# Output projection of a conv and mLSTM encoder: cross products with 16-bit operands, their narrow copies made by ScalarE

## The chip, the core and the metric

The kernel runs on one core of one Trainium2 chip. The metric is the device time of one execution, in microseconds (us); lower is better.

## What is computed

One layer of an encoder on two token groups (256 and 1024 tokens of width 1024): a short gated convolution beside a bidirectional mLSTM, one output projection, and a mixture of 16 experts with expert choice. The change touches the output projection alone:

```python
mlstm_out = jax.nn.sigmoid(o) * ht.reshape(bsz, s, V_W)
mix = jnp.concatenate([conv_out, mlstm_out], axis=-1)
return x + jnp.einsum('bse,ed->bsd', mix, w_out)      # then rms_norm, router, top-k, experts
```

## The kernel before

Five engines run one hand-written program each, in a fixed order, and meet at semaphores. The work has three stages.

1. Input projection (to about 370 us). Each float32 operand is split: a high part rounded to fp32r and a low part (the rest). A product is high x high plus two cross products (high x low, low x high). The cross products of this stage take bf16 operands (`hn_nar`, `wnar`), whose narrow high copies ScalarE makes (line 922).
2. The scan (about 350 to 550 us) over NT = 10 tiles of 128 tokens. For tile n, TensorE makes scores and numerators of the mLSTM, ScalarE scales one direction (`hb`, line 1167), VectorE adds the two (`ht`, line 1614), ScalarE takes their squares (`junkh`, line 1178), VectorE the roots and the gated product `mix`; TensorE transposes `mix` into PSUM (line 2095). ScalarE rounds the high parts of the mix, `conv_high` for slices 0 to 3 (from `cvs`, line 1081) and `heads_high` for slices 4 to 7 (line 1086); VectorE makes the low parts, `conv_low` and `heads_low` (lines 1623, 1651). `project(n, h, k0, k1)` (line 2013) multiplies slices k0 to k1 of tile n with half h of w_out, 512 columns at a time. It is called in pieces, one tile behind the numerators: twelve matmuls a piece in tile 0 (four pieces), then pieces of 2, 2, 4 slices a half. The result `x1` (VectorE's `residual`, line 1556, or ScalarE's `residual_out`, line 1135) is transposed (line 2035), copied to `xT` by ScalarE (line 1094), and multiplied with the router (lines 2050, 2057); token squares are ScalarE's `junk` (line 1109). From tile 8 on VectorE runs the top-k (`choose`).
   w_out is split too: `out_high(k)` on ScalarE (line 1073) and `out_low(k)` on VectorE (line 1573), slices 0 to 3 before the loop, 4 to 7 inside tile 0.
3. The experts (from about 569 us), bound by TensorE and the transfer of the weights.

The order on each engine is that in which the code is written. ScalarE's loop over n calls, for 2 <= n < 8: token_squares(n-2), columns_out(n-2, 1), hb(n), conv_high(n), logit_parts(n-2), squares of the heads (n), softmax_terms, exponentials(n+2), columns_out(n-1, 0), heads_high(n). The inner loop of `project` is this:

```python
for a, (x, w) in enumerate(((xh, wh), (xh, wl), (xl, wh))):
    mm = pe.matmul(psum[:, 6 + h, :], x, w,
                   start=(k == 0 and a == 0), stop=(k == KD - 1 and a == 2 and not with_x))
```

## Time and profile before

| | |
|---|---|
| runs shown | 1290.13, 1288.26, 1289.65 us; median 1289.65 |
| profiled execution | 1287.62 us, span 1285.9 us |
| TensorE matmul busy | 1249.5 us (97%) |
| VectorE, ScalarE, GpSimd busy | 904.5 us (70%), 743.2 us (58%), 320.9 us (25%) |
| mean granted TensorE clock | 0.992 |
| chain that ended last | TensorE 91%, VectorE 3%, issue 2%, ScalarE 2% |
| line 2013 (output projection) | 480 matmuls, 9% of the chain |

The page lists busy time per engine, the chain of work that ended last, and the costliest groups. In a timeline each row is a start, a length, the engine, the line, and what is written from what. Matmuls overlap, so the distance between starts tells the cost of one, not its length.

### The profile page before, as it was taken

How to read it: one execution, taken by the hardware profiler on the slowest of the kernel's cores; microseconds unless marked ns; L12 is line 12 of the kernel's file. 1: busy time of each engine (PE TensorE's matmuls, PEld its weight loads, DVE VectorE, ACT ScalarE, POOL GpSimd, SP SyncE). 2: the span in 40 equal slices, each digit the busy share in tenths (PEclk: the TensorE clock that was granted, in tenths of full speed). 3: DMA queues.
4: the chain of work that ended last, by engine and by line, in shares of the span. 5: the costliest groups of instructions: out<-in, count | busy, mean ns of one | idle time of the engine just before them, and what ended most of it. 6: DMA issues, size and time to landing. Idle time of an engine off the chain costs nothing.

```text
span 1285.9 us, 25128 instructions
## 1 busy us (share of the span) xinstructions
PE 1249.5 (97%) x9766; PEld 1026.7 (80%) x9818; DVE 904.5 (70%) x1293; ACT 743.2 (58%) x1082; POOL 320.9 (25%) x316
## 2 busy tenths in 40 slices
PE   8999999999999999889999999999999999999994
PEld 7868996666688888678988898888889888988893
DVE  6462122442487555989888887888798889888887
ACT  7645322223345454468667766766776667667765
POOL 2512221010143331141232213231314131223040
PEclk9999999999999999989999999999999999999997
DMA  8231544360279774199999999999999999999997
GB/s 276 67 123 51 167 145 129 119 178 10 94 214 283 213 210 138 56 304 369 346 305 311 316 338 297 310 325 333 296 318 333 319 301 316 344 303 309 296 347 282
DMA packets 242176, 314.76 MB, mean 245 GB/s; under 512 B 16112, under 2 KB 206064, under 8 KB 242112
## 3 DMA queue, kind: packets, MB, share of 16 engines
q1 hardware_dynamic: 226720, 268.54, 63.4%
q0 software_dynamic: 15392, 45.36, 12.0%
q8 instruction: 42, 0.69, 0.2%
q14 instruction: 22, 0.18, 0.1%
HBM read 274.41 MB, written 39.44 MB: 244 GB/s over the span
## 4 chain that ended last, share of the span: by engine, by line
PE 91%; DVE 3%; issue 2%; ACT 2%; DMA 1%; POOL 1%; SPq 0%; POOLq 0%; ACTq 0%; DVEq 0%
PE psum L2301 23%; PE psum L2162 15%; PE psum L2308 11%; PE psum L2013 9%; PE psum L2324 9%; PE psum L2129 8%; PE psum L2342 4%; PE psum L2333 4%; PE psum L2075 1%; PE psum L2294 1%; PE psum L2080 1%; PE psum L2035 1%; PE psum L1993 1%; PE psum L2027 1%; DVE eraw L1919 1%
## 5 line engine op out<-in xcount | busy, mean ns | idle before, releaser
L1846 DVE TENSOR_TENSOR elo<-eraw,ehi 128x2048 bf16<-128x2048 f32 x192 | 433.2, 2283 | 1.2 <-ACT ehi L1240 1.2
L1240 ACT ACTIVATE ehi<-eraw 128x2048 fp32r<-128x2048 f32 x192 | 362.2, 1902 | 22.5 <-PE psum L2342 17.3
L2301 PE MATMUL psum<-xc,ehi 128*128 128x320 f32 x2048 | 330.4, 313 | 1.5 <-DVE xc L1851 1.5
L2301 PEld LDWEIGHTS psum<-xc,ehi 128*128 128x128 f32 x2048 | 302.3, 188 | 3.0 <-DVE xc L1851 1.8
L2308 PE MATMUL psum<-xb,elo 128*128 128x160 bf16 x2048 | 163.9, 233 | 0.0
L1859 DVE TENSOR_REDUCE gu<-psum 128x320 f32<-128x640 f32 x128 | 104.9, 820 | 78.0 <-PE psum L2308 77.9
L2308 PEld LDWEIGHTS psum<-xb,elo 128*128 128x128 bf16 x2048 | 138.5, 98 | 13.1
L2162 PE MATMUL psum<-hn_nar,wnar 128*128 128x512 bf16 (+1 forms) x748 | 141.2, 343 | 1.2
L2324 PE MATMUL psum<-ehi,hc 128*128 128x512 f32 x512 | 132.6, 406 | 0.0
L2162 PEld LDWEIGHTS psum<-hn_nar,wnar 128*128 128x128 bf16 x768 | 73.0, 98 | 63.0 <-issue 4.5
L2324 PEld LDWEIGHTS psum<-ehi,hc 128*128 128x128 f32 x512 | 95.1, 188 | 22.2
L1402 DVE SCALAR_TENSOR_TENSOR wnar<-wraw,g1c,whi 128x256 bf16<-128x256 f32 x96 | 40.0, 486 | 100.6 <-ACT whi L930 100.5
L1304 ACT ACTIVATE sg<-gu 128x320 f32<-128x320 f32 x64 | 30.2, 472 | 135.8 <-DVE gu L1859 135.8
L2129 PE MATMUL psum<-hn_hi,whi 128*128 128x512 f32 (+1 forms) x384 | 83.6, 367 | 0.0
L824 POOL DMA_INDIRECT acc_s<-yt,idx x15 | 24.1, 1605 | 222.8 <-ACT yp L1261 192.9
L2129 PEld LDWEIGHTS psum<-hn_hi,whi 128*128 128x128 f32 x384 | 63.5, 188 | 12.1 <-issue 0.3
L2162 PE MATMUL psum<-wnar,hn_nar 128*128 128x256 bf16 (+1 forms) x608 | 71.7, 274 | 1.0 <-DVE hn_nar L1377 0.6
L930 ACT ACTIVATE whi<-wraw,g1c 128x256 fp32r<-128x256 f32 x92 | 38.0, 496 | 50.1 <-PE psum L2129 48.6
L2013 PE MATMUL psum<-woh,mxh 128*128 128x512 f32 x160 | 66.5, 416 | 0.2 <-ACT xT L1094 0.2
L2162 PEld LDWEIGHTS psum<-wnar,hn_nar 128*128 128x128 bf16 x608 | 57.7, 98 | 9.7 <-issue 1.0
L2013 PE MATMUL psum<-woh,mxl 128*128 128x512 f32 x160 | 62.7, 392 | 0.0
L2013 PE MATMUL psum<-wol,mxh 128*128 128x512 f32 x160 | 62.4, 390 | 0.0
(294 smaller groups left out, 1652.8 us busy)
## 6 DMA issues: line engine op xcount, KB each, us to landing
eraw<-in_w_gate_dram SPq DMA_DIRECT2D x64, 1024.0 KB, 9.6
eraw<-in_w_up_dram SPq DMA_DIRECT2D x64, 1024.0 KB, 8.1
eraw<-in_w_down_dram SPq DMA_DIRECT2D x64, 1024.0 KB, 12.5
wraw<-in_w_in_dram SPq DMA_DIRECT2D x12, 1024.0 KB, 7.4
negm<-negm_d SPq DMA_DIRECT2D x10, 512.0 KB, 6.9
v<-v_d SPq DMA_DIRECT2D x18, 256.0 KB, 4.0
xa<-in_x_sample_dram SPq DMA_DIRECT2D x8, 512.0 KB, 6.8
xs<-in_x_sample_dram SPq DMA_DIRECT2D x8, 512.0 KB, 5.0
```

The lines of the kernel that those rows point to most:

```text
L1240: act.activation(f["ehi"][:, j % RING, :], f["eraw"][:, raw_slot(s, j), :], ACT.Copy).then_inc(S["ehi"], 1)
L1402: w = dve.scalar_tensor_tensor(wnar[j % 2][:, LOW, k, 0:CH], b["wraw"][:, j % 2, k, :], b["g1c"][:, k:k + 1], whi[j % 2][:, k, 0:CH].bitca ...
L1846: dve.tensor_tensor(f["elo"][:, j % RING, :], f["eraw"][:, raw_slot(s, j), :], f["ehi"][:, j % RING, :].bitcast(F32), ALU.subtract).then_i ...
L1859: dve.tensor_reduce(f["gu"][:, (i // 2) % 2, i % 2, :, :], both, AX_X, ALU.add).then_inc(S["gu_add"], 1)
L2013: mm = pe.matmul(psum[:, 6 + h, :], x, w, start=(k == 0 and a == 0), stop=(k == KD - 1 and a == 2 and not with_x))
L2129: mm = pe.matmul(result(i), lhs, rhs, start=(first and k == 0), stop=(not first and k == KD - 1))
L2162: mm = pe.matmul(result(i), lhs, rhs, start=(first and k == 0 and of_x == LOW), stop=(not first and k == KD - 1 and of_x == HIGH))
L2301: pe.matmul(o[:, 0:2 * NC], hi[:, k, c], x[:, k, :, :].rearrange("p a t -> p (a t)"), start=(k == 0), stop=False, skip_group_check=True)
L2308: mm = pe.matmul(o[:, NC:2 * NC], lo[:, k, c], xb[:, k, :], start=False, stop=(k == KD - 1), skip_group_check=True)
L2324: mm = pe.matmul(psum[:, 4 + h, :], f["hc"][:, 2 * q + kk, a, :], f["ehi"][:, j % RING, full_columns(kk, h)], start=(q == 0 and kk == 0 an ...
L2333: pe.matmul(psum[:, 4 + h, :], f["hbf"][:, 2 * q + kk, :], f["elo"][:, j % RING, full_columns(kk, h)], start=False, stop=False, skip_group ...
L2342: mm = pe.matmul(psum[CAPP * i:CAPP * (i + 1), 6, 0:CH], f["hid"][:, k, CAPS:NC], f["eraw"][:, raw_slot(s, j), c], start=(k == 0), stop=(k ...
```

## The change

The low parts of w_out and of the mix become bf16, and a narrow bf16 copy of each high part is added beside them: `wol` becomes `won` and `mxl` becomes `mxn`, each with room for both in the same bytes. ScalarE makes the narrow copies: `out_weights_narrow(k)` eight times (128x1024) and `mix_narrow(n, k0)` twice a tile (128x512). In `project` all high products of a call come first, then all its cross products, with waits for the narrow copies between. The high products and the number of matmuls stay as they are.

```diff
@@ -230,14 +230,14 @@
         d = {}
-        for specs in ([("mxh", [P, KD, T], F32R), ("mxl", [P, KD, T], F32R)],
-                      [("woh4", [P, KD, T], F32R), ("wol4", [P, KD, T], F32R)],
+        for specs in ([("mxh", [P, KD, T], F32R), ("mxn", [P, KD, 2 * T], BF16)],
+                      [("woh4", [P, KD, T], F32R), ("won4", [P, KD, 2 * T], BF16)],
                       [("cvs", [P, KD, T], F32), ("woraw4", [P, KD, T], F32)]):
             d.update(stage_buffers(specs))
         d.update(overlay(size(HN[:1]), ("og", [P, KD, T], F32)))
         d.update(overlay(at_weights, ("woraw0", [P, 4, D], F32)))
-        d.update(overlay(at_weights, ("wol0", [P, 4, D], F32R)))
+        d.update(overlay(at_weights, ("won0", [P, 4, 2 * D], BF16)))
         d.update(overlay(at_weights + 2 * SLOT, ("woh0", [P, 2, D], F32R)))
         d.update(overlay(at_weights + 3 * SLOT + WIDE, ("woh2", [P, 2, D], F32R)))
@@ -264,7 +264,7 @@
         QUARTERS = SP_ // KD
         spare_col = d["router"][:, 2, SP_ - 1:SP_]
         mxh = d["mxh"][:, 2:4, SP_:T].rearrange("p s (k t) -> p s k t", k=KD)
-        mxl = d["mxl"][:, 0:2, SP_:T].rearrange("p s (k t) -> p s k t", k=KD)
+        mxn = d["mxn"][:, 0:2, 2 * SP_:2 * T].rearrange("p s (a k t) -> p s a k t", a=2, k=KD)
         cvs = d["cvs"][:, 1, SP_:T].rearrange("p (s k t) -> p s k t", s=2, k=4)
         og = d["og"][:, 2, SP_:T].rearrange("p (s n) -> p s n", s=2)
         g2b = d["g2b"][:, :]
@@ -279,9 +279,9 @@
                 return d[("woh0", "woh2")[k // 2]][:, k % 2, :]
             return d["woh4"][:, k, SP_:T]
-        def out_lo(k):
-
-            return d["wol0"][:, k, :] if k < 4 else d["wol4"][:, k, SP_:T]
+        def out_narrow(k, a):
+
+            return d["won0"][:, k, a * D:(a + 1) * D] if k < 4 else d["won4"][:, k, 2 * SP_ + a * D:2 * SP_ + (a + 1) * D]
         HALF2, PROMPT = 32, 64
         SEL = PROMPT + NE
@@ -1073,6 +1073,17 @@
                 act.activation(out_hi(k), out_raw(k), ACT.Copy, scale=d["hgc"][:, k - 4:k - 3] if k >= 4 else 1.0
                                ).then_inc(S["wo_hi"], 1)
+            def out_weights_narrow(k):
+
+                act.wait_ge(S["wo_lo"], k + 1)
+                act.activation(out_narrow(k, HIGH), out_hi(k).bitcast(F32), ACT.Copy).then_inc(S["wo_nar"], 1)
+
+            def mix_narrow(n, k0):
+
+                act.wait_ge(S["mxh_done"], 2 * n + (1 if k0 == 0 else 2))
+                act.activation(mxn[:, n % 2, HIGH, k0:k0 + 4, :], mxh[:, n % 2, k0:k0 + 4, :].bitcast(F32), ACT.Copy
+                               ).then_inc(S["mx_nar"], 1)
+
             def conv_high(n):
                 act.wait_ge(ld_mix[n % 2], 16 * 2 * (n // 2 + 1))
@@ -1140,6 +1151,8 @@
                 out_high(k)
             for n in range(3):
                 exponentials(n)
+            for k in range(4):
+                out_weights_narrow(k)
             for n in range(NT + 2):
                 if n == NT:
@@ -1167,10 +1180,16 @@
                         i = act.activation(d["hb"][:, h, :], psum[:, 3 + h % 2, VPAD * (h // 2):VPAD * (h // 2) + DV],
                                            ACT.Copy, scale=d["sm"][:, n % 2, 4 + by_half(h):5 + by_half(h)])
                     i.then_inc(S["hb_done"], 1)
+                    if n == 1:
+                        for k in range(4, KD):
+                            out_weights_narrow(k)
+                        mix_narrow(0, 4)
                     if n >= 1:
                         conv_high(n)
                     if n >= 2:
                         logit_parts(n - 2)
+                    if n >= 1:
+                        mix_narrow(n, 0)
                     act.wait_ge(S["ht_done"], n + 1)
                     if n >= 1:
                         act.wait_ge(S["hsum"], n)
@@ -1180,6 +1199,7 @@
                     i.then_inc(S["hsum"], 1)
                     if n == 0:
                         conv_high(0)
+                        mix_narrow(0, 0)
                         for k in range(4, KD):
                             out_high(k)
                 if n == NT - 1:
@@ -1196,6 +1216,8 @@
                     columns_out(n - 1, 0)
                 if n < NT:
                     heads_high(n)
+                    if n > 0:
+                        mix_narrow(n, 4)
                 if n == NT - 1:
                     residual_out(n - 1, 1)
                     scaled_tokens(LATE)
@@ -1570,7 +1592,7 @@
             def out_low(k):
                 dve.wait_ge(S["wo_hi"], k + 1)
-                dve.scalar_tensor_tensor(out_lo(k), out_raw(k), d["hgc"][:, k - 4:k - 3] if k >= 4 else 1.0,
+                dve.scalar_tensor_tensor(out_narrow(k, LOW), out_raw(k), d["hgc"][:, k - 4:k - 3] if k >= 4 else 1.0,
                                          out_hi(k).bitcast(F32), ALU.mult, ALU.subtract).then_inc(S["wo_lo"], 1)
             def router_weights():
@@ -1620,7 +1642,7 @@
                 s = n % 2
                 dve.wait_ge(S["mxh_done"], 2 * n + 1)
-                dve.tensor_tensor(mxl[:, s, 0:4, :], cvs[:, s, :, :], mxh[:, s, 0:4, :].bitcast(F32), ALU.subtract
+                dve.tensor_tensor(mxn[:, s, LOW, 0:4, :], cvs[:, s, :, :], mxh[:, s, 0:4, :].bitcast(F32), ALU.subtract
                                   ).then_inc(S["cvl_done"], 1)
             def head_roots(n):
@@ -1648,7 +1670,7 @@
             def heads_low(n):
                 dve.wait_ge(S["mxh_done"], 2 * n + 2)
-                dve.tensor_tensor(mxl[:, n % 2, 4:8, :], psum[:, 5, :].rearrange("p (k t) -> p k t", k=4),
+                dve.tensor_tensor(mxn[:, n % 2, LOW, 4:8, :], psum[:, 5, :].rearrange("p (k t) -> p k t", k=4),
                                   mxh[:, n % 2, 4:8, :].bitcast(F32), ALU.subtract).then_inc(S["mxl_done"], 1)
             def last_roots():
@@ -2002,16 +2024,24 @@
                     pe.wait_ge(S["xT_done"], 2 * (n - 1) + h + 1)
                 c = slice(512 * h, 512 * h + 512)
                 with_x = joint(n) and (n, h) != (NS, 0)
+                if n == 0:
+                    pe.wait_ge(S["wo_hi"], k1)
+                if k1 == KD:
+                    pe.wait_ge(S["mxh_done"], 2 * n + 2)
                 for k in range(k0, k1):
-                    if n == 0:
-                        pe.wait_ge(S["wo_lo"], k + 1)
-                    if k == 4:
-                        pe.wait_ge(S["mxl_done"], n + 1)
-                    xh, xl = mxh[:, n % 2, k, :], mxl[:, n % 2, k, :]
-                    wh, wl = out_hi(k)[:, c], out_lo(k)[:, c]
-                    for a, (x, w) in enumerate(((xh, wh), (xh, wl), (xl, wh))):
-                        mm = pe.matmul(psum[:, 6 + h, :], x, w,
-                                       start=(k == 0 and a == 0), stop=(k == KD - 1 and a == 2 and not with_x))
+                    pe.matmul(psum[:, 6 + h, :], mxh[:, n % 2, k, :], out_hi(k)[:, c], start=(k == 0), stop=False)
+                if n == 0:
+                    pe.wait_ge(S["wo_lo"], k1)
+                    pe.wait_ge(S["wo_nar"], k1)
+                if k0 == 0:
+                    pe.wait_ge(S["mx_nar"], 2 * n + 1)
+                if k1 == KD:
+                    pe.wait_ge(S["mxl_done"], n + 1)
+                    pe.wait_ge(S["mx_nar"], 2 * n + 2)
+                for k in range(k0, k1):
+                    for of_x, of_w in ((HIGH, LOW), (LOW, HIGH)):
+                        mm = pe.matmul(psum[:, 6 + h, :], mxn[:, n % 2, of_x, k, :], out_narrow(k, of_w)[:, c], start=False,
+                                       stop=(k == KD - 1 and of_x == LOW and not with_x))
                 if k1 == KD:
                     if with_x:
                         pe.wait_ge(ld_x[n % 2], 16 * (n // 2 + 1))
```

TensorE, the start of tile 0's projection: four transposes of the heads, the scores of tile 2, then two pieces. Before (operands w_out high or low, mix high or low; two slices of the first piece):

```order
L2027 MATMUL psum<-qz,kTs 128x128 x4
L2013 MATMUL psum<-woh,mxh 128x512
L2013 MATMUL psum<-wol,mxh 128x512
L2013 MATMUL psum<-woh,mxl 128x512
L2013 MATMUL psum<-woh,mxh 128x512
L2013 MATMUL psum<-wol,mxh 128x512
```

Now (all four pieces of tile 0, up to the numerators of tile 2):

```order
L2057 MATMUL psum<-qz,kTs 128x128 x4
L2032 MATMUL psum<-woh,mxh 128x512 x4
L2043 MATMUL psum<-won,mxn 128x512 x8
L2032 MATMUL psum<-woh,mxh 128x512 x4
L2043 MATMUL psum<-won,mxn 128x512 x8
L2032 MATMUL psum<-woh,mxh 128x512 x4
L2043 MATMUL psum<-won,mxn 128x512 x8
L2032 MATMUL psum<-woh,mxh 128x512 x4
L2043 MATMUL psum<-won,mxn 128x512 x8
L2105 MATMUL psum<-vs,SD 128x129 x8
```

The triples are sorted into runs of four high and eight cross products; each run of eight stands behind the waits for `wo_lo`, `wo_nar`, `mx_nar` and, in the third piece, `mxl_done`.

ScalarE from the squares of tile 0 to those of tile 1. Before:

```order
L1178 ACTIVATE junkh,ms<-ht 128x128 x4
L1081 ACTIVATE mxh<-cvs 128x512
L1073 ACTIVATE woh<-woraw,hgc 128x1024 x4
L1086 ACTIVATE mxh<-psum 128x512
L1167 ACTIVATE hb<-psum,sm 128x128 x4
L1081 ACTIVATE mxh<-cvs 128x512
L1178 ACTIVATE junkh,ms<-ht 128x128 x4
```

Now:

```order
L1197 ACTIVATE junkh,ms<-ht 128x128 x4
L1092 ACTIVATE mxh<-cvs 128x512
L1084 ACTIVATE mxn<-mxh 128x512
L1073 ACTIVATE woh<-woraw,hgc 128x1024 x4
L1097 ACTIVATE mxh<-psum 128x512
L1180 ACTIVATE hb<-psum,sm 128x128 x4
L1079 ACTIVATE won<-woh 128x1024 x4
L1084 ACTIVATE mxn<-mxh 128x512
L1092 ACTIVATE mxh<-cvs 128x512
L1084 ACTIVATE mxn<-mxh 128x512
L1197 ACTIVATE junkh,ms<-ht 128x128 x4
```

Between `hb(1)` and the squares of tile 1 stand four copies of 128x1024 and two of 128x512 more than before.

ScalarE in the last tile, n = 9. Before:

```order
L1094 ACTIVATE xT<-psum 128x512
L1086 ACTIVATE mxh<-psum 128x512
L1135 ACTIVATE x<-psum 128x512
L1117 ACTIVATE tk<-x,ms 128x1024
L1094 ACTIVATE xT<-psum 128x512
```

Now:

```order
L1105 ACTIVATE xT<-psum 128x512
L1097 ACTIVATE mxh<-psum 128x512
L1084 ACTIVATE mxn<-mxh 128x512
L1146 ACTIVATE x<-psum 128x512
L1128 ACTIVATE tk<-x,ms 128x1024
L1105 ACTIVATE xT<-psum 128x512
```

The narrow copy of the last four slices stands between the high copy and the residual `x`.

## Rows read from the trace of the kernel before

**Rows 1.** The page: busy time of TensorE (section 1) and the chain (section 4).
```profile
PE 1249.5 (97%) x9766; PEld 1026.7 (80%) x9818; DVE 904.5 (70%) x1293; ACT 743.2 (58%) x1082; POOL 320.9 (25%) x316
...
PE 91%; DVE 3%; issue 2%; ACT 2%; DMA 1%; POOL 1%; SPq 0%; POOLq 0%; ACTq 0%; DVEq 0%
```

**Rows 2.** Windows, one round of the scan; us, busy of PE, PEld, DVE, ACT, POOL, clock, DMA.
```profile
439.75:457.00 17.25, 17.25 (x121) 14.44 (x120) 10.40 (x36) 8.74 (x29) 5.29 (x8) 1.00 0.74 214
```

**Rows 3.** Timeline of TensorE, tile 0; columns: start, length, instruction.
```profile
376.45 0.39 PE L2013 MATMUL psum<-wol,mxh 128*128 128x512 f32 x1
...
380.31 0.39 PE L2013 MATMUL psum<-woh,mxh 128*128 128x512 f32 x1
...
385.75 0.94 PE L2075 MATMUL psum<-vs,SD 128*128 128x129 f32 x7
```

**Rows 4.** Runs of bf16 (timeline) and fp32r products (chain) before the scan.
```profile
359.99 3.40 PE L2162 MATMUL psum<-hn_nar,wnar 128*128 128x512 bf16 x15
```

```profile
348.82 3.68 PE psum L2129 x16
```

**Rows 5.** Timelines of ScalarE and VectorE in tile 0.
```profile
376.99 1.15 ACT L1073 ACTIVATE woh<-woraw,hgc 128x1024 fp32r<-128x1024 f32 x1 [0.41 <-DMA woraw<-in_w_out_dram]
...
378.52 1.14 ACT L1167 ACTIVATE hb<-psum,sm 128x128 f32<-128x128 f32 x4
...
384.00 0.31 ACT L1178 ACTIVATE junkh<-ht 128x128 f32<-128x128 f32 x1 [3.09 <-DVE ht L1614]
```

```profile
379.26 2.47 DVE L1573 SCALAR_TENSOR_TENSOR wol<-woraw,hgc,woh 128x1024 fp32r<-128x1024 f32 x2
```

**Rows 6.** ScalarE copies: a run in the timeline, and one form of the groups.
```profile
339.25 3.90 ACT L1073 ACTIVATE woh<-woraw 128x1024 fp32r<-128x1024 f32 x4 [21.01 <-PE psum L2129]
```

```profile
L922 ACT ACTIVATE wnar<-whi 128x2048 bf16<-128x2048 f32 x12 | 22.9, 1910 | 0.3
```

**Rows 7.** The chain in tile 1; columns: start, length, what.
```profile
390.98 0.60 ACT xT L1094
...
393.64 0.64 PE psum L2050 x16
```

**Rows 8.** Timelines of ScalarE, VectorE and TensorE in a steady round.
```profile
430.57 0.18 ACT L1178 ACTIVATION_READ_ACCUMULATOR junkh<-ht 128x1 f32 x1
...
443.41 0.60 ACT L1094 ACTIVATE xT<-psum 128x512 f32<-128x512 f32 x1 [1.83 <-PE psum L2035]
```

```profile
430.94 0.17 DVE L1356 TENSOR_SCALAR ms<-ms 128x5 f32<-128x5 f32 x1
...
434.49 0.68 DVE L1556 TENSOR_TENSOR x<-psum,xs 128x512 f32<-128x512 f32 x1
```

```profile
436.10 0.60 PE L2035 MATMUL psum<-ident,x 128*128 128x128 f32 x4
```

**Rows 9.** Timelines of ScalarE and VectorE in the last tile.
```profile
526.95 0.60 ACT L1086 ACTIVATE mxh<-psum 128x512 fp32r<-128x512 f32 x1 [3.44 <-PE psum L2095]
527.44 0.59 ACT L1135 ACTIVATE x<-psum 128x512 f32<-128x512 f32 x1
```

```profile
521.31 0.28 DVE L1796 COPY AFF<-psum 16x128 f32<-16x128 f32 x1
```

**Rows 10.** Windows of TensorE (busy, clock, DMA), and its first instruction behind two stops.
```profile
526.90:528.10 1.20, 0.02 (x2) 1.00 0.00 0
543.00:546.00 3.00, 0.95 (x16) 1.00 0.56 176
...
547.00:555.00 8.00, 5.38 (x29) 0.57 1.04 349
...
1271.00:1272.00 1.00, 0.54 (x2) 0.73 1.03 418
```

```profile
549.76 0.60 PE L2268 MATMUL psum<-ident,aff 128*16 128x128 f32 x2 [2.62 <-DVE aff L1675]
```

```profile
1271.44 0.54 PE L2399 MATMUL psum<-spare 128*128 128x1 f32 x2 [2.06 <-ACT psum L1338]
```

More of the change, by code:

```diff
@@ L339, in hybrid_conv_mlstm_moe @@
             "ld0 ld1 ldm0 ldm1 ld_mix0 ld_mix1 ld_x0 ld_x1 padded qs_done s_ps e_exp e_done sd_done num_ps router "
-            "den_done hb_done ht_done hsum mix_done mixT_ps mxh_done mxl_done o_ps x1_done "
+            "den_done hb_done ht_done hsum mix_done mixT_ps mxh_done mxl_done wo_nar mx_nar o_ps x1_done "
             "x1_out0 x1_out1 sum2 tk_done tk_out0 tk_out1 xT_ps2 xT_done "
```

## Prediction

> **What bounds the kernel now.** I read the page first, then the chain of waits, then each engine's timeline in the scan stage, the only stage that the change touches. TensorE is busy for 97% of the span and makes 91% of the chain that ended last [rows 1]: the reader should see that a microsecond of TensorE time is worth a microsecond nearly everywhere. One round of the scan (17.25 us) has TensorE busy for all of it, ScalarE for 8.74 and VectorE for 10.40 [rows 2]. So work can be added to ScalarE for nothing, but only where nobody stands waiting for the instruction behind it. There are three places in the scan where somebody does.
>
> **Part 1, the cross products.** There are 10 tiles x 2 halves x 8 slices x 2 = 320 of them. In the middle of a run of full-width fp32r products TensorE starts one every (385.75 - 376.45) / 41 = 0.2268 us [rows 3]. The same shape in bf16 runs elsewhere in this kernel: 15 records in 3.40 us from the first start to the last end, where one takes 0.379, so (3.40 - 0.38) / 14 = 0.216 us [rows 4]. That gives 320 x 0.011 = 3.5 us. The busy means (about 390 against 379 ns) would say the same; the pitch is what counts, since matmuls overlap. The 160 high products now start in runs of 2 or 4 right behind 16-bit ones; a run of 16 such in the input projection goes at 3.68 / 16 = 0.230 us [rows 4], so they lose 160 x 0.003 = 0.5. I take **-3.0 us**. Ends: -3.5 if the high ones keep 0.2268; -2.4 if besides the first cross product behind each high run keeps the fp32r pitch (4 + 9 x 6 = 58 runs x 0.011 = 0.6).
> The rows show fp32r at 227 and bf16 at 216 ns. The Trainium skill (TensorE: Matmul & The Clock Gate, Back-to-back issue gap) gives a warm isolated gap of N / 2.4 + 2.5 ns whatever the type, 216 ns at 512 columns; by that alone this part would be worth nothing, and the trace agrees only for bf16.
>
> **Part 2, the copies that TensorE waits for.** In tile 0 the order is: hb(1), then the four narrow copies of w_out slices 4 to 7, then the narrow copy of the four head slices of mix, and the third call of project (half 0, slices 4 to 7) needs all five before its first cross product. ScalarE starts hb(1) at 378.52 and is through with issuing it at 379.52 (four instructions of 1.14 in all, the last overlapping by 0.14) [rows 5]. A copy of 128x1024 costs (3.90 - 1.05) / 3 = 0.95 us in a run [rows 6]; a bf16 result makes it no faster (128x2048 takes 1.910) [rows 6]. VectorE has the last low part ready at 379.26 + 2.47 = 381.73 [rows 5], before the fourth copy would start at 379.52 + 3 x 0.95 = 382.37. Then the mix copy starts at 383.3 and takes 0.63: **ready at 383.9**. TensorE reaches the third call at 380.31 [rows 3], less 16 x 0.011 = 0.2, and its four high products take 0.9: **it is there at 381.05**. It stands still for **+2.9 us**. Nothing of TensorE's can pass the wait: 20 matmuls and the next round's numerators (385.75 [rows 3]) are queued behind it. Ends: +2.3 (only the last copy and the mix copy behind the low part of 381.73: 1.05 + 0.5), +3.7 (each copy at 1.15, the length of one with a scale column [rows 5]).
>
> **Part 3, the same copies on the way to the squares.** conv_high(1) and the first narrow copy of tile 1 stand behind those five. VectorE's head sums are done at 384.0, where ScalarE's squares start [rows 5]; now conv_high starts at 383.8, its narrow copy 0.65 later, and the squares 0.5 after that, at 385.0. That is 1 us later on a path that has to meet a TensorE 2.7 us later: free. The four copies for slices 0 to 3 wait for VectorE's low parts and end some 0.4 us after ScalarE would have begun hb(0); the last eviction of the stage waits for TensorE, so this is free too.
>
> **Part 4, one link in tile 1.** The chain from TensorE's transposes at 390.98 to the router product at 393.64 is all ScalarE: xT, mxh, junk, xT [rows 7]. The narrow copy of tile 1's head slices now stands between mxh and junk. It waits for mxh's own completion, 0.1, and issues for 0.5: **+0.6 us**. Ends 0.5 and 0.75.
>
> **Part 5, the steady rounds.** The copy ahead of the squares delays them by 0.4; they ended at 430.75 and VectorE began the roots at 430.94 (it waits for the logits as well), so 0.2 us reach it. The residual behind the roots is there at 434.49 + 0.68 = 435.17, and TensorE takes it up 0.9 us later [rows 8]: covered. The copy ahead of junk uses up 0.6 of the 1.83 us that ScalarE waits for xT [rows 8]. Cost 0; if that cover were gone it would be up to 0.6 a round.
>
> **Part 6, one link at the end.** In the last tile mxh at 526.95 is followed at once by x (residual, 527.44), for which TensorE's transposes wait [rows 9]. The narrow copy goes between: **+0.6 us**. VectorE's top-k chain began at 521.31 when TensorE's affinities came [rows 9]; the two chains reach the first gather within some 0.2 us of each other. So the 0.6, less the 0.4 that TensorE gains on its last 66 matmuls, is seen in full.
>
> **Sum without the clock:** -3.0 + 2.9 + 0.6 + 0.6 = +1.1 us. VectorE's instructions, the queues of SP and GpSimd and all transfers keep their order and sizes; they only shift.
>
> **Part 7, the clock.** The granted clock fell to its lower level, 1.2 of 2.4 GHz, twice here: at 547.8, after a stretch of few and small products (busy 0.95 of the 3 us from 543), and at about 1271.45, when TensorE had stood still for 2.06 us behind dense work [rows 10]. Idle spells of 1.2 us (526.9 [rows 10]) left it alone. The new stop of 2.9 us is longer than the one that was followed by a fall. A mean of 0.57 over the eight microseconds from 547 [rows 10] is 6.8 us at half speed, from 547.8 to 554.7 or 4.9 us beyond TensorE's return at 549.76. Ends: 0, and 4.9 / 2 = 2.5 us. I take 2.8 us of busy low time, so **+1.4 us**, since what resumes here are full-width products and not 128-column transposes.
> The Trainium skill (TensorE: Matmul & The Clock Gate, Why this matters for your kernels) asks for no idle gaps over about 3 us between bursts; by that the gap of 2.9 just escapes and the sum stays +1.1. This speaks for rival B.
>
> **The cases.** A change of 0.2% is 2.6 us; less than that can't be told from none. The profiled execution took 1287.62 us (span 1285.9), 2.0 under the median of 1289.65; I add the sum to the median.
> - **A, forecast, 0.42:** the stop and one short fall of the clock, +2.5: **1292.1 us**. It lies just under the bound, so about half of its chance is slower.
> - **B, the stop without a fall, 0.25:** +1.1: 1290.8. For it: nothing shows that every stop of 2 us brings a fall. Against: the 2.06 us before 1271.44.
> - **C, the clock stays low for long, 0.13:** the other side, slower. Place: the stop at 381 to 384. It decides if the low level lasts as long as it did behind 549.76: 1.1 + 2.5 = +3.6, and +4.6 if the copies take 1.2 us each: 1293.3 to 1294.3.
> - **E, ScalarE becomes the bound in the steady rounds, 0.08:** if the two copies a round reach TensorE by 0.5 us each in 8 rounds, +4.0 on top of 1.1: 1294.8. From 1.83 us of wait down to nothing it would take three times the copy that I count; against.
> - **D, the gain without the stop, 0.10:** if ScalarE's copies are over before TensorE is there (each 128x1024 under 0.3 us), only -3.0 + 1.2 = -1.8; together with a pitch of 0.216 for the high products as well (160 x 0.014 = 2.2 and 0.5 more), -4.5: 1285.2. Nothing in rows 6 supports copies that fast.
> - The change doing something else than it says (0.02) is out by the order of instructions: 320 products of mxn with won are there.
>
> Faster by over 0.2%: D without its smaller half and a little for what I do not see, 0.09. Slower: half of A, C, E, 0.40. Within: 0.51. The range takes A, B and C with the bounds of parts 1, 2 and 7: 1288.3 to 1294.5.
>
> **What would show it.** Right: cross products at 379 ns and 0.216 apart; TensorE idle once for about 2.9 us near 381, released by ScalarE's narrow copy of mix; the granted clock under 1.00 within 3 us of that; in later rounds no wait of TensorE, and a round of about 16.95 us; 28 more ScalarE copies, 8 of some 1.04 and 20 of some 0.6 us. Wrong: a stop under 1.5 us or none; rounds that don't get shorter (the pitch was not the type's), or longer ones (E); a wait for wo_lo in place of the copies.

## The result and the profile after

| | before | after |
|---|---|---|
| median of 13 runs each | 1288.15 us | 1292.54 us |
| range of them | 1287.58 to 1290.13 | 1290.74 to 1294.45 |
| ratio, 95% interval | | 1.0029 [1.0022, 1.0037] |
| profiled execution, its span | 1287.62, 1285.9 | 1292.54, 1290.8 |

The change makes the kernel slower: by 0.29% or 3.7 us by the ratio, by 4.4 us between the two medians. Twice more, on other occasions, the ratio was 1.0022 and 1.0026.

The page of after, sections 1, 4 and 5 (against [rows 1]):

```profile
PE 1251.7 (97%) x9818; PEld 994.4 (77%) x9818; DVE 904.6 (70%) x1293; ACT 761.5 (59%) x1110; POOL 320.6 (25%) x316
...
PE 89%; DMA 3%; DVE 3%; ACT 2%; issue 2%; POOL 1%; SPq 0%; POOLq 0%; ACTq 0%; DVEq 0%
...
L2043 PE MATMUL psum<-won,mxn 128*128 128x512 bf16 x320 | 80.0, 384 | 3.0 <-ACT mxn L1084 3.0
```

The first row has 28 more ScalarE instructions and 18 us more of its time, while weight loads lose 32 us. The chain has 3% DMA, which before had 1%; three transfers are new in it, and two of them are shown below. The last row is the group of the cross products: its one idle time is a stop of 3.0 us for the narrow copy of mix.

TensorE's timeline in tile 0 (against [rows 3]):

```profile
381.20 1.28 PE L2032 MATMUL psum<-woh,mxh 128*128 128x512 f32 x4
385.51 2.68 PE L2043 MATMUL psum<-won,mxn 128*128 128x512 bf16 x8 [3.03 <-ACT mxn L1084]
387.63 2.27 PE L2032 MATMUL psum<-woh,mxh 128*128 128x512 f32 x4
```

Four high products take 1.28 us ahead of the stop and 2.27 behind it, so the clock fell. Windows of after across that place, and one steady round; us, busy of PE, PEld, DVE, ACT, POOL, granted clock, DMA (against [rows 2]):

```profile
386.00:387.00 1.00, 1.00 (x5) 0.39 (x4) 0.61 (x1) 1.00 (x5) 0.00 (x0) 0.73 1.32 167
387.00:390.00 3.00, 3.00 (x8) 1.67 (x7) 1.88 (x12) 3.00 (x14) 0.00 (x0) 0.52 1.03 348
390.00:391.00 1.00, 1.00 (x6) 0.49 (x5) 0.96 (x3) 0.05 (x1) 0.88 (x2) 1.00 1.12 344
428.31:445.24 16.93, 16.93 (x120) 11.10 (x119) 10.40 (x36) 9.76 (x31) 5.28 (x8) 1.00 0.79 219
```

The clock is at its lower level, 1.2 of 2.4 GHz, from about 386.5 to 390. The round is 16.93 us instead of 17.25, TensorE busy for all of it, although ScalarE has 1.0 us more to do.

The way to the stop, in the chain of waits of after:

```profile
12.07 7.41 DMA xa<-in_x_sample_dram
...
368.84 9.54 DMA woraw<-in_w_out_dram
...
379.46 0.57 ACT mxh L1097
380.04 1.03 ACT hb L1180 x4
381.07 3.78 ACT won L1079 x4
384.85 0.53 ACT mxn L1084
...
385.51 2.68 PE psum L2043 x8
```

The chain of after has 36.8 us of DMA, that of before 16.6. The transfer of w_out is 9.5 of them and leads to the stop: ScalarE runs without a pause from its landing to the fifth copy, and TensorE stands behind it. The first row shown is another matter. The input x lands at 19.5 us, after ScalarE has waited 0.8 us for it, and TensorE then waits 1.47 us for ScalarE's `hn_hi` at 23.8, against 0.34 at 22.6 in before. From there on this execution runs 1.2 us late, long before the first line that the change touches (the third of the new transfers, 7.9 us of `wraw`, stands before this one).

ScalarE in tile 1 (against [rows 7]) shows the link:

```profile
397.06 0.59 ACT L1097 ACTIVATE mxh<-psum 128x512 fp32r<-128x512 f32 x1
397.69 0.63 ACT L1084 ACTIVATE mxn<-mxh 128x512 bf16<-128x512 f32 x1
398.22 1.04 ACT L1120 ACTIVATE junk<-x 128x1024 f32<-128x1024 f32 x1
```

Before, mxh at 391.48 was followed by junk at 391.95, 0.47 us later. Now it is 1.16.

**Stages of the program.** From the timelines I took when TensorE begins each tile's numerators (tile 1: T1), the first router product, the last projection, and GpSimd's first gather of rows for the experts (`xg`). Each difference is a stage, in us:

| kernel | T1 | T1 to T2 | to router | to T3 | T3 to T9 | to last projection | to gather | to end |
|---|---|---|---|---|---|---|---|---|
| before | 370.47 | 15.28 | 7.89 | 11.59 | 103.50 | 32.98 | 20.05 | 724.14 |
| after | 371.69 | 19.83 | 8.36 | 11.49 | 101.58 | 33.08 | 20.35 | 724.44 |
| difference | +1.22 | +4.55 | +0.47 | -0.10 | -1.92 | +0.10 | +0.30 | +0.30 |

The differences add up to 4.9 us, the difference of the two spans. T1 to T2 holds the stop and the fall of the clock; the six rounds from T3 to T9 give back 0.32 us each. The first column is the late landing of x; it and the last column were in no part of the prediction.

### The profile page after: what moved, and what is told of

The parts are those of the page before. It is cut to its first block, busy times and chain, and to the rows that moved or that the text cites. A ratio compares the mean times of both kernels' runs of the same rounds, so it can differ in the third digit from the quotient of the medians.

```text
span 1290.8 us, 25232 instructions
## 1 busy us (share of the span) xinstructions
PE 1251.7 (97%) x9818; PEld 994.4 (77%) x9818; DVE 904.6 (70%) x1293; ACT 761.5 (59%) x1110; POOL 320.6 (25%) x316
## 4 chain that ended last, share of the span: by engine, by line
PE 89%; DMA 3%; DVE 3%; ACT 2%; issue 2%; POOL 1%; SPq 0%; POOLq 0%; ACTq 0%; DVEq 0%
PE psum L2331 23%; PE psum L2192 15%; PE psum L2338 11%; PE psum L2354 9%; PE psum L2159 8%; PE psum L2043 5%; PE psum L2372 4%; PE psum L2363 4%; PE psum L2032 3%; PE psum L2324 1%; PE psum L2105 1%; PE psum L2110 1%; DMA woraw<-in_w_out_dram 1%; PE psum L2065 1%; PE psum L2015 1%
## 5 line engine op out<-in xcount | busy, mean ns | idle before, releaser
L2192 PE MATMUL psum<-hn_nar,wnar 128*128 128x512 bf16 (+1 forms) x768 | 143.8, 344 | 0.0
L2043 PE MATMUL psum<-won,mxn 128*128 128x512 bf16 x320 | 80.0, 384 | 3.0 <-ACT mxn L1084 3.0
L2363 PE MATMUL psum<-elo,hbf 128*128 128x512 bf16 x256 | 66.4, 382 | 0.0
L2372 PE MATMUL psum<-eraw,hid 128*32 128x256 f32 x1024 | 61.9, 382 | 0.0
```

The costliest lines, as they stand in the source:

```text
L2043: mm = pe.matmul(psum[:, 6 + h, :], mxn[:, n % 2, of_x, k, :], out_narrow(k, of_w)[:, c], start=False, stop=(k == KD - 1 and of_x == LOW a ...
L2192: mm = pe.matmul(result(i), lhs, rhs, start=(first and k == 0 and of_x == LOW), stop=(not first and k == KD - 1 and of_x == HIGH))
L2363: pe.matmul(psum[:, 4 + h, :], f["hbf"][:, 2 * q + kk, :], f["elo"][:, j % RING, full_columns(kk, h)], start=False, stop=False, skip_group ...
L2372: mm = pe.matmul(psum[CAPP * i:CAPP * (i + 1), 6, 0:CH], f["hid"][:, k, CAPS:NC], f["eraw"][:, raw_slot(s, j), c], start=(k == 0), stop=(k ...
```

## Experiments

Each kernel's expectation stands as it was recorded. All ratios are to the kernel before on the same chip. The stage to T3 is left out here: 11.50 to 11.60 us.

| kernel | median us | ratio, 95% interval | T1 | T1 to T2 | to router | T3 to T9 | to last proj. | to gather | to end |
|---|---|---|---|---|---|---|---|---|---|
| types_only | 1287.89 | 0.9985 [0.9976, 0.9994] | 370.96 | 15.75 | 7.71 | 101.56 | 32.45 | 20.74 | 725.73 |
| copies_only | 1295.73 | 1.0056 [1.0041, 1.0070] | 370.47 | 21.45 | 8.36 | 103.48 | 33.67 | 19.96 | 724.13 |
| ungrouped | 1295.09 | 1.0047 [1.0034, 1.0060] | 370.60 | 22.19 | 8.36 | 102.48 | 33.30 | 20.17 | 724.58 |
| fill | 1293.64 | 1.0037 [1.0025, 1.0049] | 370.73 | 18.21 | 8.37 | 101.58 | 33.10 | 20.67 | 725.86 |
| change_again | 1292.08 | 1.0022 [1.0011, 1.0032] | 371.42 | 20.28 | 8.36 | 101.56 | 33.10 | 20.59 | 725.89 |
| links | 1290.93 | 1.0015 [1.0006, 1.0024] | 372.83 | 20.63 | 7.70 | 101.56 | 32.45 | 20.79 | 726.05 |
| nostop | 1289.09 | 0.9998 [0.9989, 1.0007] | 370.62 | 16.45 | 9.77 | 101.58 | 33.10 | 19.95 | 724.77 |
| both | 1288.04 | 0.9989 [0.9980, 0.9998] | 371.00 | 16.12 | 8.58 | 101.56 | 32.45 | 20.60 | 724.54 |
| fill_again | 1293.67 | 1.0034 [1.0022, 1.0046] | 370.47 | 18.37 | 8.36 | 101.56 | 33.11 | 20.27 | 727.27 |
| change_third | 1292.91 | 1.0026 [1.0017, 1.0035] | 371.29 | 17.80 | 8.36 | 101.58 | 33.09 | 19.95 | 725.84 |
| both_again | 1288.70 | 0.9993 [0.9984, 1.0002] | 371.32 | 15.66 | 8.60 | 101.56 | 32.46 | 20.59 | 724.43 |
| before_again | 1289.34 | 1.0002 [0.9992, 1.0012] | 370.40 | 15.28 | 8.14 | 103.48 | 32.99 | 20.00 | 724.17 |

### The two halves of the change: types_only and copies_only

types_only has the change's order and 16-bit operands, but no narrow copies and no waits for them. Its cross products multiply the low part of mix with the low part of w_out in both places, so this part of the projection is another sum.

```diff
-for k in range(4): out_weights_narrow(k)
-mix_narrow(...)
-pe.wait_ge(S["wo_nar"], k1); pe.wait_ge(S["mx_nar"], ...)
-pe.matmul(..., mxn[:, n % 2, of_x, k, :], out_narrow(k, of_w)[:, c], ...)
+pe.matmul(..., mxn[:, n % 2, LOW, k, :], out_narrow(k, LOW)[:, c], ...)
```

> The changed kernel without ScalarE's narrow copies and their waits; both cross products multiply the low parts (low x low), so the cross products are left out of the result while their number, shape and type stay. Theory (the gain is the 16-bit pitch, the loss is the copies): no stop near 381, the clock stays at its upper level there, each steady round 16.93 us against 17.25, and the whole is 3.0 to 3.5 us faster than before (ratio 0.9973 to 0.9977). Rival (16-bit products or their grouping cost something themselves, such as a slower high product or a slower start behind a wait): equal to before or slower, ratio 1.000 or more.

copies_only is the kernel before with the change's order, copies and waits; the copies go to memory that nobody reads (ScalarE's squares also wait for the first of them, which are long done), and all products stay fp32r.

```diff
+for k in range(4): out_weights_narrow(k)   # and all other calls, as in the change
-pe.matmul(..., mxn[:, n % 2, of_x, k, :], out_narrow(k, of_w)[:, c], ...)
+pe.matmul(..., (mxh, mxl)[..., k, :], (out_lo, out_hi)(k)[:, c], ...)   # fp32r
```

> The kernel before with all products in fp32r, high ones first in each call as in the change, and the 28 narrow copies made by ScalarE at the same places into unused memory, with the same waits of TensorE. Theory: the stop near 381 is there with 2.8 to 3.1 us, in most executions the clock falls behind it (1.7 us), the link in tile 1 (0.5) and the one in the last tile (0.6) too; rounds stay at 17.25 us; 5.5 to 7 us slower than before. Rival (the copies are hidden, the loss has to do with the 16-bit operands): within 2 us of before.

The two halves come apart in the table. The types alone give the whole gain of the rounds (101.56 against 103.50) and neither link (7.71 and 32.45). The copies alone leave the rounds at 103.48, so ScalarE's copies of 0.63 us, two a round, cost the steady rounds nothing; the copies carry the stop (21.45) and both links (8.36, and 33.67 against 32.98).

The expectation for types_only, 3.0 to 3.5 us faster than before, was missed: the ratio gives 1.9 us (0.8 to 3.1). Its trace shows why. From T1 to the last projection it takes 168.97 us against 171.24, 2.3 less, and that holds a wait of 0.56 us in tile 0 for VectorE's low part of w_out that before doesn't have; so the shorter products are worth 2.8 us up to there. From T9 to the gather it takes 53.19 us against 53.03: the 0.5 us gained on the last tile is not seen at the gather (see links). copies_only, 7.2 us slower by the ratio (5.3 to 9.0), was expected at 5.5 to 7. The stop, in the waits of TensorE from 350 to 600 us of copies_only, and the clock behind it:

```profile
PE psum L2066 <- ACT free L1104: 3.0, 1, 3.0
```

```profile
383.00:391.00 8.00, 6.62 (x17) 5.20 (x18) 5.91 (x23) 5.89 (x20) 1.28 (x2) 0.57 1.10 299
```

Eight microseconds at a mean of 0.57 are a low stretch twice as long as in after, and T1 to T2 is 1.6 us longer than in after.

### Grouping: ungrouped

```diff
-for k in range(k0, k1):
-    pe.matmul(psum[:, 6 + h, :], mxh[...], out_hi(k)[:, c], ...)
 ...
 for k in range(k0, k1):
+    pe.matmul(psum[:, 6 + h, :], mxh[...], out_hi(k)[:, c], ...)
     for of_x, of_w in ((HIGH, LOW), (LOW, HIGH)):
```

> The changed kernel with the old order inside a call: high, cross, cross for each slice. The waits for the copies come before the first high product. Theory (a product behind one of the other type takes the fp32r pitch, and high products ahead of the stop are work done in its shadow): rounds of 17.05 us or more (10 more changes of type a round at 0.011), the stop 0.9 us longer, 1.8 to 2.0 us slower than the change. Rival (order of the types is free): rounds as in the change, 16.93 us, and only the 0.9 us of the stop.

The wait of TensorE (its waits from 350 to 575 us) is 1.6 us longer than in after:

```profile
PE psum L2040 <- ACT mxn L1084: 4.6, 1, 4.6
```

Four high products that no longer run ahead of it make 0.9 of that, as expected. The other 0.7, which was not, is when things came: T1 is 1.1 us earlier than in after and the last slice of w_out 0.4 earlier.

The rounds tell more. With each fp32r product between 16-bit ones they take 102.48 / 6 = 17.08 us against 16.93 grouped and 17.25 with one type. Grouped, a round has its 16 high products in 6 runs (pieces of 2 or 4 slices), ungrouped in 16, so 10 more turns from one type to the other and back cost 0.15 us, some 0.015 each. Grouping is worth nearly half of what the types give.

### The clock behind the stop: fill, fill_again, change_again and change_third

fill keeps TensorE busy in the stop with 24 transposes to PSUM columns that nobody reads any more.

```diff
 if n == 0:
+    if (h, k0) == (0, 4):
+        pe.wait_ge(S["mxl_done"], 1)
+        for _ in range(24):
+            pe.transpose(psum[:, 5, 384:512], ident[:, :], ident[:, :])
     pe.wait_ge(S["wo_lo"], k1)
```

> The changed kernel with 24 transposes of the identity into an idle bank between the high and the cross products of the third piece of tile 0, some 2.6 us of work that nobody needs, so that TensorE is not idle while it waits. Theory (the fall of the clock is caused by the stop and costs 1.7 us of the loss): the granted clock stays 1.00 from 380 to 395, the first cross product starts at the same time behind ScalarE's copy, and the whole is 1.2 to 1.7 us faster than the change; 2 us slower than before. Rival (the fall is beside the point, since what it slows is waited for anyway): same as the change, 3.7 us slower than before.

> The changed kernel once more, beside the three below on one chip. Theory: from the numerators of tile 1 to those of tile 2 it takes 18.2 us if the clock holds, 19.8 with one short fall and 21.4 with a long one, in this profile too, and which of them comes is chance; time 3 to 4.5 us over before. Rival (the fall is tied to the program, not to the moment): again one fall of 3.4 us behind the stop, 19.8 us.

> The changed kernel with 24 transposes in the stop, a second time, beside the change itself on the same chip. Theory (the fall of the clock behind the stop costs 1.6 us and the transposes take it away): 1.6 us under the change in the median. Rival (what the fall costs is won back or lost again at the start of the experts, where some executions have a second low stretch of about 1.5 us, by chance): no difference, or up to 1 us over the change. In the profile: no granted clock under 1.00 from 375 to 405 us; tile 1's numerators to tile 2's 18.2 us against 19.8 to 20.3.

> The change unaltered, for the comparison with the transposes in the stop. Theory: 3.0 to 4.0 us over before, as in the first result. A ratio of 1.002 to 1.0035. In the profile a stop of 3 to 4 us ahead of the first cross product of tile 0's third call and a low stretch of the clock behind it; a second low stretch near 571 us in some executions.

TensorE of fill at that place, and the clock in the window behind it:

```profile
381.36 2.78 PE L2037 MATMUL psum<-ident 128*128 128x128 f32 x24
384.56 1.89 PE L2047 MATMUL psum<-won,mxn 128*128 128x512 bf16 x8 [0.41 <-ACT mxn L1084]
```

```profile
384.00:390.00 6.00, 5.59 (x32) 3.42 (x31) 3.91 (x17) 5.07 (x19) 0.83 (x2) 1.00 1.13 272
```

The clock stays at 1.00, the eight cross products take 1.89 us instead of 2.68, and T1 to T2 is 1.6 us shorter than in after (18.21 against 19.83). So within the scan the short fall costs 1.6 us. Yet fill is not the 1.2 to 1.7 us faster than the change that was expected: both its medians stand at or above the change's (1.0034 against 1.0026 on the same chip). Two things in the traces speak to that.

The first is change_third, which is the change itself. Its TensorE at the stop, and the clock behind it:

```profile
384.69 1.89 PE L2043 MATMUL psum<-won,mxn 128*128 128x512 bf16 x8 [2.62 <-ACT mxn L1084]
```

```profile
384.00:388.00 4.00, 3.31 (x15) 1.78 (x16) 2.16 (x10) 3.97 (x17) 0.00 (x0) 1.00 1.14 239
```

A stop of 2.62 us, less than the 3 to 4 us expected, was followed by no fall: T1 to T2 is 17.80, 2.5 over before. Those of 3.0 (after, copies_only), 3.5, 4.0 (links) and 4.6 us (ungrouped) were. change_again, at 20.28, is after with a stop 0.44 us longer and the same short fall. In three traces the change thus had the fall twice, and transposes can only save what an execution without them would have lost.

The second is far behind the change, at the first products of the experts, which take 2.62 us in before. Here is the one group of 16 in the timelines of before, change_third and fill:

```profile
569.12 2.62 PE L2301 MATMUL psum<-xc,ehi 128*128 128x320 f32 x16 [1.54 <-DVE xc L1851]
```

```profile
570.86 4.10 PE L2331 MATMUL psum<-xc,ehi 128*128 128x320 f32 x16 [1.40 <-DVE xc L1873]
```

```profile
571.45 4.09 PE L2335 MATMUL psum<-xc,ehi 128*128 128x320 f32 x16 [1.21 <-DVE xc L1873]
```

In six of the fourteen profiled executions the clock was low near 570 us, and all six have 725.7 us or more in the last column (types_only, both of fill, change_again, change_third, links); the other eight have 724.1 to 724.8. That is 1.5 us, the price of the fall at 386, and both profiled executions of fill paid it. What brings it on was not settled. Neither the copies nor the stop are needed for it, since types_only has it, nor do they bring it each time: after, copies_only, ungrouped and nostop don't have it.

Each execution without a trace has its mean granted clock on record, and that says more. Of the 92 executions of before that have it, 49 had 0.992 or more (mean time 1288.6 us) and 43 had 0.991 or less (1290.0). types_only, nostop and the two of both had 0.992 or more in 22 of 45, the change, with its fall at 386 in some or most of them, in none of 32. fill has no fall at 386 any more, yet none of its 12 executions reached 0.992. So they had low time elsewhere, and more often than before has; that the transposes bring it on is not shown.

### The links: links

The copy of the last four slices of mix moves behind the work that TensorE waits for.

```diff
-if n >= 1: mix_narrow(n, 0)          # before the head squares
+if n >= 2: mix_narrow(n - 1, 4)      # before logit_parts(n - 2)
 ...
+if n >= 1: mix_narrow(n, 0)          # behind the head squares
 ...
-if n > 0: mix_narrow(n, 4)           # behind heads_high(n)
+if n == NT: mix_narrow(n - 1, 4)     # last tile: behind the token squares
```

> The changed kernel with ScalarE's narrow copies of the mix moved off the two links: that of slices 0 to 3 behind the squares of the heads, that of slices 4 to 7 of tile n into tile n+1 behind conv_high (for the last tile behind the token squares). The copies of w_out stay. Theory: the stretch from the numerators of tile 2 to the first router product shrinks from 8.36 to 7.8 us or less, the wait of the transposes for ScalarE's x in the last tile from 1.8 to 1.2 us, rounds stay at 16.93; the stop of 3.0 stays, so 1.0 to 1.2 us faster than the change. Rival (what stands on the links is hidden by TensorE's own lateness): those two stretches unchanged, time as the change.

ScalarE in tile 1 of links has nothing between mxh and junk:

```profile
398.99 0.59 ACT L1097 ACTIVATE mxh<-psum 128x512 fp32r<-128x512 f32 x1
399.47 1.06 ACT L1120 ACTIVATE junk<-x 128x1024 f32<-128x1024 f32 x1
```

T2 to the router product is 7.70 against 8.36 and T9 to the last projection 32.45 against 33.10: 0.65 us each, where the theory had them. The ratio fell from 1.0022 to 1.0015 on one chip, 0.9 us of the 1.3, with intervals that overlap.

The first 0.65 us is kept: the stage to T3 stays 11.50. The second is kept in small part. From T9 to the gather the four traces of 16-bit kernels without the copy in the link take 53.05 to 53.24 us (mean 53.13), the six with it and with grouped products 53.04 to 53.77 (mean 53.39), before 53.03. The wait of GpSimd's first `tk` behind the scan, in change_third and in links, says what else stands there:

```profile
551.90 2.37 POOL L738 TENSOR_TENSOR tk<-tk,g2b 128x1024 f32<-128x1024 f32 x1 [5.51 <-ACT tk L1128]
```

```profile
555.29 2.37 POOL L738 TENSOR_TENSOR tk<-tk,g2b 128x1024 f32<-128x1024 f32 x1 [5.86 <-DVE aff L1698]
```

Without the copy in the link the work waits for VectorE, whose top-k fills the last tile; in types_only and both the chain that ends last runs through it from 512 us on. In this pair GpSimd starts 0.3 us earlier after T9 (41.07 against 41.36), and nothing of that is left at the gather.

The profiled execution of links had a stop of 4.0 us and T1 2.4 us late, for reasons that are not in the edit. Its clock was low from 25.3 to 28.8 us, which costs 1.6 of the 2.4 us:

```profile
26.00:27.00 1.00, 1.00 (x6) 0.61 (x5) 0.59 (x3) 0.68 (x3) 1.00 (x2) 0.50 0.78 152
```

The last two slices of w_out were copied from 379.26 on.

### Without the stop: nostop, both, both_again

ScalarE copies mix first and the w_out slices after conv_high(1). TensorE does the eight high products of both halves first, then takes slice by slice, both halves, each behind its own wait.

```diff
 if n == 1:
-    for k in range(4, KD): out_weights_narrow(k)
     mix_narrow(0, 4)
 conv_high(n)
+if n == 1:
+    for k in range(4, KD): out_weights_narrow(k)
 ...
-project(0, 0, 4, KD)      # and project(0, 1, 4, KD)
+project_rest()            # 8 high products; then per k: wait_ge(S["wo_nar"], k + 1), 4 cross products
```

> The changed kernel with tile 0 rearranged: TensorE makes the high products of slices 4 to 7 for both halves first, then the cross products slice by slice for both halves, each slice waiting for its own copy only; ScalarE copies the mix and makes conv_high(1) ahead of the four copies of w_out. The narrow copies of the mix stand where the change has them. Theory: the copies (one each 0.95 us from 381) run in step with 0.86 us of cross products a slice, the stop goes down from 3.0 to 0.5 us or less, no fall of the clock there; numerators of tile 1 to those of tile 2 in 15.0 to 15.6 us; 4 us faster than the change, within 1 us of before. Rival (the stop only moves: squares, roots and mix of tile 1 are 1 us later, and TensorE then stands before the transposes): that stretch 15.5 us, but the next one, to the first router product, 9 us or more, so half of the gain at most.

> Both rearrangements together. Theory: 15.0 to 15.6 us from the numerators of tile 1 to those of tile 2, 7.6 to 8.0 to the router product, six rounds in 101.6 us, no wait over 1.3 us at the end; 2 to 3 us faster than before (ratio 0.998), 6 us faster than the change. Rival (one of the two covers the other): no better than the first or the second alone.

> The version without the stop and with both links taken out, on this chip: 0.5 to 2.5 us under before (ratio 0.998 to 0.9996) if its gain is that of the types less what the copies of w_out still cost in tile 0; 1.000 if the first result was the chip's scatter.

TensorE of nostop in tiles 0 and 1:

```profile
380.44 2.08 PE L2059 MATMUL psum<-woh,mxh 128*128 128x512 f32 x8
383.46 3.78 PE L2067 MATMUL psum<-won,mxn 128*128 128x512 bf16 x16 [0.93 <-ACT won L1079]
387.07 1.95 PE L2127 MATMUL psum<-vs,SD 128*128 128x129 f32 x16
...
392.32 0.63 PE L2147 MATMUL psum<-ident,mix 128*128 128x128 f32 x4 [1.11 <-DVE mix L1667]
```

The stop went from 3.0 to 0.9 us and the clock stayed up. But the squares of tile 1 on ScalarE stand behind the late copies, VectorE's roots behind the squares, and TensorE now waits 1.1 us for mix. That path was covered only as long as TensorE itself was late. So both halves of the expectation came in part: the stop is short, though not 0.5, T1 to T2 is 16.45 instead of 15.0 to 15.6, and the rival's next stage of 9 us or more is there (9.77). nostop ends level with before (0.9998), as forecast. With the links taken out too, both is faster than before in one comparison (0.9989 [0.9980, 0.9998]) and not separable from it in the other (0.9993 [0.9984, 1.0002]): some 1.1 us, half of the 2 to 3 us expected of both and less than types_only has. What is missing is T1 to T2 and the router stage, 24.26 to 24.70 us together against 23.46.

### A second trace of before: before_again

> The kernel before, unaltered, for a second trace of it: how far do its stages differ from one execution to the next? Theory (about 1 us at the start of the scan and 1.5 us between the first gather and the end are scatter that any execution can have): tile 1's numerators 0.3 to 1 us later than 370.47, w_out's last slices copied later than at 376.99, and in some executions a second low stretch of the clock near 570 us. Rival (the change itself brings both): tile 1's numerators within 0.2 us of 370.47, w_out's last slice at 377.0, 724.1 us from the first gather to the end. Rounds of the scan 17.25 us and ratio 1.000 either way.

All stages but one repeat within 0.1 us (the router's is 0.25 longer); T1 is 370.40 and the last column 724.17. So two traces of before show neither a late start nor the low stretch near 570 us, as the rival had it, but the rival's cause is not borne out for the start: fill_again, with the change's code, begins tile 1 at 370.47. In all fourteen traces the lateness of T1 against before is there, within 0.1 us, by 32 us already, ahead of everything that the change touches; in after, change_again, types_only and links the chain leads there from the landing of x. The last slice of w_out in before_again was copied at

```profile
377.17 1.15 ACT L1073 ACTIVATE woh<-woraw,hgc 128x1024 fp32r<-128x1024 f32 x1 [0.42 <-DMA woraw<-in_w_out_dram]
```

against 376.99 in the first trace [rows 5] and, in the changed kernels,

```profile
378.41 1.15 ACT L1073 ACTIVATE woh<-woraw,hgc 128x1024 fp32r<-128x1024 f32 x1 [0.32 <-DMA woraw<-in_w_out_dram]
```

```profile
377.59 1.15 ACT L1073 ACTIVATE woh<-woraw,hgc 128x1024 fp32r<-128x1024 f32 x1 [0.42 <-DMA woraw<-in_w_out_dram]
```

in after and in change_third. The stops were 3.0 and 2.6 us. From the last copy to the stop ScalarE never idles, so each microsecond by which this transfer is late reaches TensorE, less what TensorE is late itself (T1). Starting from after, the stop should be 3.03 + (start of the last slice's copy - 378.41) - (T1 - 371.69). For change_third that gives 3.03 - 0.82 + 0.40 = 2.61 (measured 2.62); for change_again, whose last copy began at 378.57, 3.46 (3.47); for links, 380.52, 4.00 (4.02). So the scatter of the stop is that of the landing against T1. In before TensorE had no stop there.

## Why the prediction was right or wrong

The case came out as forecast A: the stop, one short fall of the clock in the recorded profile, and a net loss. The predicted 1292.1 us is 0.4 under the measured 1292.54. The agreement is partly luck, since the sum was +2.5 over a median of three runs of 1289.65, while thirteen runs give 1288.15 and a difference of 3.7 by the ratio, 4.4 by the medians. The lower end of the range, 1288.3, doesn't follow from the bounds that it names: with -3.5, +2.3, +0.6, +0.6 and no fall the sum is 0.0, so 1289.65.

- **Part 1** (-3.0): right in cause and size. The rounds lose 0.32 us each in every kernel with grouped 16-bit cross products, and up to the last projection it is 2.8 us in all (types_only, less its wait of 0.56). The loss of high products behind 16-bit ones, which I took from one row, is there too; it shows in ungrouped as 0.015 us for each turn of type. By the Trainium skill's gap, which knows no type (TensorE: Matmul & The Clock Gate, Back-to-back issue gap), there would have been no gain; the rounds speak against that.
- **Part 2** (+2.9, ends 2.3 and 3.7): right in place, releaser and size: 3.03, 3.47 and 2.62 us in three traces of the change. The copies cost what was said: 381.07 to 384.85 is 0.945 each. In after the copies were ready at 385.4 instead of 383.9, and TensorE came at 382.5 instead of 381.05; 1.2 of both is the late start of the whole program, so the difference held. What I missed is that ScalarE's end also moves with the landing of w_out, TensorE's only with T1. I had fixed the landing at 376.99; against T1 it moved by -0.4 to +0.4 us between the three traces, and the stop with it.
- **Part 3** (free): right for the change, and for the reason given, that TensorE is later still. nostop shows the price once that cover is gone: 1.1 us.
- **Part 4** (+0.6): 0.66, shown by links.
- **Part 6** (+0.6, "seen in full"): 0.65 up to the last projection, and 0.60 at the gather where the products gain nothing beside it (copies_only, 53.63 from T9 against 53.03). In the change the 0.5 us gained on this tile nearly cancels it. VectorE's top-k is as close as the prediction said, and that it didn't carry on: without the link those 0.5 us would not reach the gather either (types_only, 53.19).
- **Part 5** (0): right. copies_only has rounds of 17.25 with all copies in them. Rival E is out.
- **Part 7** (+1.4, ends 0 and 2.5): the size differs by execution. 1.6 us with a short low stretch (after against fill), about 3.2 in copies_only with the long one, and 0 in change_third. Rival B was therefore not a rival of A but another execution of the same kernel (change_third); the long stretch of C was seen in copies_only alone, not in the three traces of the change. The Trainium skill asks for no idle gaps over about 3 us (TensorE: Matmul & The Clock Gate, Why this matters for your kernels); the six stops of changed kernels at this place agree, with no fall behind 2.62 us and one behind each of 3.0 and more. Elsewhere a shorter gap was no protection: the 2.06 us at the end of before [rows 10] had a fall behind it, the falls near 570 us had no single wait over 1.7 us in the 10 us ahead of them, and that at 25 us in links had waits of 1.0 and 0.6 us.
- **Rival D** fell: the stop was there in every kernel with the copies in the change's order (in fill the transposes stand in it). Its 1285.2 also counts the 0.5 us of slower high products twice.
- **Not in the sum:** some 0.6 us at the start (T1 is 0 to 1.2 us later in eleven of the twelve traces of changed kernels, 2.4 in links) and the 1.5 us near 570 us. Both come in some executions only. They may be why a sum of +2.5 was measured as +3.7, but that is not shown: before has two traces, both of its faster kind (clock 0.992), and 43 of its 92 executions on record were of the slower one.

Where the gain went, then: 2.8 us of shorter products were earned up to the last projection, the last 0.5 of them in a tile where VectorE's top-k would have kept it and the link in the last tile uses it up. Paid were 3.0 for the stop, 0.65 for the link in tile 1, and up to 1.6 on top for the clock.

## What to carry to other kernels

Work given to an idle engine is free in the steady rounds and is paid for at the ends of the pipeline: price it in the first tile, where the operands have just landed, and in the last. There ask which engine comes next: a link taken out, or a product made shorter, gives back only the distance to the second chain. Before the narrow copies of a split operand are scheduled, put the high products of all halves ahead of the wait and wait slice by slice; and group products of one type, because each change between fp32r and 16-bit costs some of what the narrower type gives.

## What was not expected of the hardware

- A turn from 16-bit products to an fp32r one and back costs about 0.015 us (rounds of 17.08 against 16.93 us).
- The clock also fell in one execution at 25 us (links), for 3.4 us and at a price of 1.6, in code that all kernels share.
- The same kernel, stopped at the same instruction, had the clock fall in two traces (stops of 3.0 and 3.5 us) and not in a third (2.6 us). copies_only, stopped for 3.0 us, stayed low about twice as long as after, also stopped for 3.0.
- Keeping TensorE busy through the stop did hold the clock at that place and did not shorten the median. The low stretch near 570 us, in six of fourteen traces, costs as much; what starts it stays open.
